# Attention's keys and values in their own memory, and the group normalisation beside the first attention heads

## What is computed

```
# group B, last steps, per head
mu = hc.mean(-1, keepdims=True)
var = jnp.square(hc - mu).mean(-1, keepdims=True)
hc = (hc - mu) * lax.rsqrt(var + LN_EPS)
h = hc.transpose(0, 2, 1, 3).reshape(B, S, M_WIDTH) * norm_g
return (jax.nn.sigmoid(z.astype(f32)) * h).astype(u.dtype)
...
# group A: c is the normalised latent; keys and values come out of it by w_uk and w_uv
logits = q . key - slope * distance   (unpicked keys masked)
p = softmax(logits);  o = p . value
...
mix = jnp.concatenate([a_out, m_out], axis=-1) @ w_out[l]
h = layer_norm(DN_ALPHA * h + mix, ln1_g[l], ln1_b[l])
```

## Time and profile before

| what | value |
| --- | --- |
| median of 3 runs | 2743.13 us (2736.57 to 2743.91) |
| the profiled execution's own time | 2728.71 us |
| its span in the profile | 2726.9 us |
| its mean granted clock | 0.952 |
| PE busy / DVE / ACT / POOL | 92% / 65% / 51% / 11% of the span |

### The profile page before, as it was taken

The page is one execution under the profiler, slowest core; times in us unless marked ns, Lnnn a source line. Parts: engine busy times, 40 slices in busy tenths (PEclk is TensorE's granted clock), DMA queues, the critical chain, the costliest instruction groups (busy, mean ns, idle before and its releaser), DMA issues.

```text
span 2726.9 us, 37894 instructions
## 1 busy us (share of the span) xinstructions
PE 2496.0 (92%) x11204; PEld 1797.3 (66%) x11205; DVE 1762.2 (65%) x2804; ACT 1393.3 (51%) x2029; POOL 301.4 (11%) x233
## 2 busy tenths in 40 slices
PE   7999987898976999999999999999999999999991
PEld 3544456576543777777777777777777777777770
DVE  0476865453445655768867687668769669557596
ACT  0378525552111444647646575546557557346473
POOL 0003722002000000101101001100100100001012
PEclk9999998998995999999999999999999999999995
DMA  4100020002033555859957697667859859557583
GB/s 154 62 4 31 0 108 1 1 1 86 0 129 135 177 165 183 280 177 314 309 177 268 214 329 268 219 230 266 273 193 337 270 190 337 186 186 265 189 302 144
DMA packets 81644, 488.48 MB, mean 179 GB/s; under 512 B 13683, under 2 KB 14963, under 8 KB 30454
## 3 DMA queue, kind: packets, MB, share of 16 engines
q1 hardware_dynamic: 66512, 449.67, 46.1%
q0 software_dynamic: 13104, 34.11, 5.5%
q10 hardware_dynamic: 1974, 4.02, 0.5%
HBM read 465.42 MB, written 36.70 MB: 184 GB/s over the span
## 4 chain that ended last, share of the span: by engine, by line
PE 72%; DVE 14%; issue 9%; ACT 2%; DMA 2%; DVEq 0%; POOL 0%; POOLq 0%; ACTq 0%; SPq 0%
PE ps L777 15%; PE ps L778 14%; PE ps L779 14%; DVE wlo L1559 8%; PE ps L523 7%; PE ps L534 5%; PE ps L702 4%; PE ps L798 2%; PE ps L684 2%; PE ps L808 2%; PE ps L665 1%; PE ps L552 1%; PE ps L672 1%; PE ps L764 1%; PE ps L595 1%
## 5 line engine op out<-in xcount | busy, mean ns | idle before, releaser
L1559 DVE TENSOR_TENSOR wlo<-raw,whi 128x1024 fp32r<-128x1024 f32 x776 | 935.8, 1221 | 283.5 <-ACT whi L1065 257.3
L1065 ACT ACTIVATE whi<-raw 128x1024 fp32r<-128x1024 f32 x776 | 820.2, 1061 | 465.9 <-PE ps L779 439.6
L777 PE MATMUL ps<-whi,xhi 128*128 128x512 f32 x1440 | 595.8, 414 | 0.0
L778 PE MATMUL ps<-wlo,xhi 128*128 128x512 f32 x1440 | 575.9, 400 | 0.0
L779 PE MATMUL ps<-whi,xlo 128*128 128x512 f32 x1440 | 572.8, 398 | 0.0
L777 PEld LDWEIGHTS ps<-whi,xhi 128*128 128x128 f32 x1440 | 277.7, 193 | 97.2 <-issue 36.2
L779 PEld LDWEIGHTS ps<-whi,xlo 128*128 128x128 f32 x1440 | 278.2, 193 | 62.0
L778 PEld LDWEIGHTS ps<-wlo,xhi 128*128 128x128 f32 x1440 | 278.7, 194 | 53.0
L777 PE MATMUL ps<-whi,hhi 128*128 128x512 f32 x720 | 296.0, 411 | 0.0
L779 PE MATMUL ps<-whi,hlo 128*128 128x512 f32 x720 | 282.9, 393 | 0.0
L778 PE MATMUL ps<-wlo,hhi 128*128 128x512 f32 x720 | 280.7, 390 | 0.0
(11 more groups left out here) (312 smaller groups left out, 2686.0 us busy)
## 6 DMA issues: line engine op xcount, KB each, us to landing
raw<-in_w_gu SPq DMA_DIRECT2D x260, 1024.0 KB, 5.3
raw<-in_w_dn SPq DMA_DIRECT2D x128, 1024.0 KB
xT<-in_xT SPq DMA_DIRECT2D x2, 2048.0 KB, 15.9
raw<-in_w_out SPq DMA_DIRECT2D x2, 2048.0 KB
h1all<-in_x SPq DMA_DIRECT2D x4, 1024.0 KB, 8.0
hext<-h1all SPq DMA_DIRECT2D x8, 512.0 KB, 11.9
acc<-accst SPq DMA_DIRECT2D x8, 512.0 KB, 2.6
fin<-acc SPq DMA_DIRECT2D x2, 2048.0 KB, 13.2
```

Of the source, the lines that this page charges most:

```text
L777: pe.matmul(bank_ap, hi, whi[:, slot, col, :], start=start, stop=False)
L778: pe.matmul(bank_ap, hi, wlo[:, slot, col, :], start=False, stop=False)
L1065: act.activation(whi[:, j % 2, 2 * g:2 * g + 2, :], raw[:, (j + 2) % 3, 2 * g:2 * g + 2, :], ACT.Copy)\
L1559: dve.tensor_tensor(wlo[:, j % 2, s, :], raw[:, (j + 2) % 3, s, :], whi[:, j % 2, s, :].bitcast(f32), ALU.subtract).then_inc(lo_done, 1)
```

## The change

`Vn` goes to the memory of slot 2 of `raw` (address 32 KB instead of that of `vaug`), and `KTr` to that of `ucT`, the recurrence's input, which is dead by then. `w_gu[0]` therefore can't be loaded before attention has ended: its two halves are issued behind `bsrc`. On PE the `kt` and `V` tasks follow the recurrence at once, and the eight `mt` tasks are done at n = 6, 8, ... 20 of attention. On ACT the copies of `KTr` come ahead of the root, and the 32 normalising instructions follow two by two behind the exponential and the copy of n = 0 to 15. On DVE the copies of `Vn` come ahead of the reciprocal, and the copy of `mt` chunk c is the last thing of iteration n = 6 + 2c. POOL's program is the same.

```diff
+TURN_AT = tuple(range(6, 6 + 2 * NT, 2))
...
-        Vn = at("Vn", X + 102, [P, NT, AH * AD])
-        KTr = at("KTr", X + 118.5, [P, 4, S])
+        Vn = at("Vn", 32, [P, NT, AH * AD])
+        KTr = at("KTr", X + 86, [P, 4, S])
...
-            filled(sp, last_use[5])
-            half_slabs(0, a["w_gu"][0])
...
             sp.dma_start(bsrc[:, :], a["b_gu"]).then_inc(bias_all_in, 16)
+            half_slabs(0, a["w_gu"][0])
...
+                if n in TURN_AT:
+                    c = TURN_AT.index(n)
+                    b = opened(("mt", c))
+                    pe.wait_ge(mout, c + 1)
+                    for h in range(MH):
+                        ins = pe.transpose(b[:, h * P:(h + 1) * P], zs[:, c, h, :], ident)
+                    closes(ins, ("mt", c))
...
+                if n == 0:
+                    act.wait_ge(mnorm_in, 2)
+                for c, h in (divmod(2 * n, MH), divmod(2 * n + 1, MH)) if n < 2 * NT else ():
+                    act.activation(vaug[:, c, h, 0:MD], vaug[:, c, h, 0:MD], ACT.Identity,
+                                   scale=m_rstd[:, c, h:h + 1], bias=m_nmr[:, c, h:h + 1]).then_inc(mnormed, 1)
```

More of the change, by code:

```diff
@@ L76, in task_order @@
         o += [("U", c, q) for q in range(2) if c < NT - 1]
-    o += [("mt", c) for c in range(NT)]
     o += [("kt", m, n) for n in range(2) for m in range(4)] + [("V", t) for t in range(NT)]
@@ L85, in task_order @@
             o += [("at", n // AH - 1)]
+        if n in TURN_AT:
+            o += [("mt", TURN_AT.index(n))]
     for t in range(NT):
@@ L632, in _ @@
                     closes(ins, ("U", c, q))
[L633 to L638, removed]
             for j in range(2):
@@ L982, in _ @@
                     copy_out(("X", c, q), mst[:, h, :], b[:, 129:258], scale=gate_cols[:, 1, h * 8 + c:h * 8 + c + 1])
[L983 to L989, removed]
             for n in range(2):
@@ L992, in _ @@
                     copy_out(("kt", m, n), KTr[:, m, n * 512:(n + 1) * 512], filled(act, ("kt", m, n))[:, :])
+            act.wait_ge(mvar_done, 1)
+            act.activation(m_rstd[:, :, :], m_rstd[:, :, :], ACT.Sqrt).then_inc(mroot, 1)
             for n in range(NT * AH + 4):
@@ L1365, in _ @@
             dve.tensor_scalar(m_rstd[:, :, :], m_mv[:, :, :, 1], EPS, None, ALU.add).then_inc(mvar_done, 1)
+            for t in range(NT):
+                b = filled(dve, ("V", t))
+                frees(dve.tensor_copy(Vn[:, t, :], b[:, :]), ("V", t))
             dve.wait_ge(mroot, 1)
@@ L1370, in _ @@
                                      op0=ALU.mult, op1=ALU.mult).then_inc(mnorm_in, 1)
[L1371 to L1377, removed]
             astep = serial(dve, att_step)
@@ L1408, in _ @@
                                       att_rec[:, :].unsqueeze(2).to_broadcast([P, AH, AD]), ALU.mult).then_inc(o_copied, 1)
+                if n in TURN_AT:
+                    c = TURN_AT.index(n)
+                    b = filled(dve, ("mt", c))
+                    frees(dve.tensor_copy(catT[:, 4:8, c * P:(c + 1) * P], b[:, :].rearrange("p (h d) -> p h d", h=4)),
+                          ("mt", c))
             lstep = serial(dve, ln_step)
```

## The result

| kernel | median | ratio to before (95% interval) |
| --- | --- | --- |
| before | 2740.31 us (2736.57 to 2743.91, 6 runs) | |
| changed | 2727.55 us (2719.87 to 2729.74, 6 runs) | 0.9949 (0.9939 to 0.996) |

The change is worth 12.8 us, 0.5%; the prediction had 9.4. The time forecast was 2733.7 us; of the 6.1 us between it and the measured 2727.55, 2.8 lie in the median of before, which was 2743.13 over three runs and is 2740.31 over six. The profiled execution of the changed kernel has a span of 2724.5 us and took 2726.3, not the 2719.3 of the forecast: the profiled execution of before was a short one, as a second trace of it shows further down. The three terms are read from the two traces as distances, since the recurrence itself ends up to 4 us apart from one execution to the next (454.2 to 458.5 us in the traces of this study).

What follows compares the result with a forecast made beforehand. The prediction took the chain of waits between recurrence and output projection as the bound; 20.3 - 5.4 - 5.5 = 9.4 us gained, so 2743.1 - 9.4 = 2733.7 us, range 2726 to 2742.

Steps and rivals of the forecast that it cites:

- Term 1: Start of attention: keys follow the recurrence at once, normalisation leaves the path, first exponential comes earlier; gain of 20.3 us.
- Term 3: Wait before the projection: moved `w_gu[0]` takes DMA turns ahead of ACT's five small loads; 5.5 us lost.
- the bounds: Limits on the moved load's cost before the projection: 0 if ACT's loads pass first, 6.0 us at most.
- Term 2: Attention: normalisations and transposed blocks now lie in iterations 0 to 20; 5.4 us lost.
- the prediction's own sign: Attention, first exponential to last product: Term 2 is wrong if it grows by under 3 or over 9 us.
- 1.0 for the clock: Attention, change from tile 0 to 1: more transposes fall in the half-clock stretch, at twice their time; 1.0 us lost.
- It becomes the bound by 0.43 us for 4 pairs: Attention tile 0: ACT needs 2.66 us per pair of heads against 2.23; 1.7 us lost.
- 0.5 x 4 pairs = 2.0 us in tile 1: Attention tile 1: transposed blocks make odd exponentials 3.5 us apart in place of 3.01; 2.0 us lost.
- The hidden load: Before the projection: ACT's five loads don't wait for `w_gu`; gain 14.9 us, time 2728 us; chance 0.15.
- The blocked port: Attention: POOL's multiplications stop DVE's small step, costing 9.4 us; nothing left of the gain, about 2743 us; chance 0.25.
- the slower rival: Attention: PE's clock stays at half through tiles 2 and 3; 18 us slower than before, 2761 us; chance 0.05.

Runs made afterwards that it cites:

- The block's return: Changed kernel, but ACT's 32 normalisations stand in one block ahead of the first exponential, as before the change: 2740.42 us, ratio 0.9998.
- Load taken back: Changed kernel, but SP issues `w_gu[0]` only after ACT's five small loads have landed: 2722.31 us, ratio 0.9937.
- load alone: Kernel before, with only `w_gu[0]` moved, to behind `bsrc` instead of ahead of attention: 2744.74 us, ratio 1.0023.
- attention without guests: Kernel before, with PE waiting for ACT's five loads only ahead of the first router product; no normalisations or transposed blocks in attention: 2724.53 us, ratio 0.995.
- the two kernels with the blocks in late tiles: Changed kernel with the eight transposed blocks at n = 40 to 54: 2738.39 us; the same with DVE's copy one iteration later: 2729.06 us.
- the late wait: PE waits for ACT's five loads only ahead of the first router product: 2707.59 us on the changed kernel, 2724.53 us on the kernel before.

## Why the prediction was right, and where it was off

**Term 1** held, step by step: keys at once, 13.8 us for keys and values at full clock, both table loads beside the values, and DVE's reciprocal and shift laid bare (0.5 us, from 471.56 to 472.05; 0.6 predicted). The block's return shows that 13.3 of the 20.6 us are ACT's block with the table load behind it; the others come from the order of PE's work and the kept clock, which no run takes apart.

**Term 3** held. Load taken back and load alone show its cause and its size: 4.1 and 5.3 us in PE's wait, 5.2 and 4.6 us in the medians. That it was met to 0.1 us in the first pair of traces is luck, since the wait scatters by 2 us. The choice between the bounds, by the packets and not the bytes, was right: nearly all of `w_gu` went by before `br` was through, not the 1.33 MB that equal turns in bytes would allow. That the queues take turns packet by packet is what the Trainium skill, DMA: Bandwidth & Descriptors, section on queues, rings and completion order, says; the 273 and 279 packets of the two queues agree.

**Term 2** is the step that was mis-sized: 5.4 predicted, 3.2 against the first trace of before and 1.4 against the others. By the prediction's own sign (attention longer by under 3 us) it was wrong against all but the first trace. By tiles 0, 1 and 2 attention lost 2.2, 0.9 and 0.1 us against the first trace and 1.1, 0.1 and 0.1 against the second; 1.9, 2.0 and 0.5 were predicted, and 1.0 for the clock. Three parts of it:

- "It becomes the bound by 0.43 us for 4 pairs" in tile 0: true only of the first pair (0.56 us). The other pairs ran at half clock, where PE sets 2.85 us, above ACT's 2.66. The same 2.85 stands in attention without guests. The first trace of before, whose clock stayed at full for 7.3 us behind the first exponential, was the exception among the four traces with that attention (2.6 to 3.1 us in the others), and I took it for the rule. That the sum for tile 0 comes near the measured 2.2 us is luck: most of that is the clock.
- "0.5 x 4 pairs = 2.0 us in tile 1": from one odd exponential to the next, from n = 9 on, it is 3.49, 3.54, 3.41 and 3.56 us, as worked out (3.5). But the 3.01 us that I set against it was one pair of the four; before, they took 3.67, 3.50, 3.01 and 3.47. Only that one pair lost clearly, 0.4 us, and by its transposed block: in the two kernels with the blocks in late tiles it takes 3.05 us. Why the others were long before as well was not taken apart.
- The price of one transposed block isn't a constant: 0.2 us for five of them from n = 12 to 24, 1.46 us each in tiles 5 and 6. Had the change put them late, my sum of PE's time would have missed two thirds of it.

The overall step is thus one of reading: a pair is costed against the rows of its own place, and a single trace doesn't show where the clock falls in the next execution.

**The rivals.** The hidden load fell with the two load experiments. What the prediction held against it, that ACT's packets at the program's start were large, doesn't follow from its rows: 0.98 MB in 720 packets is 1.4 KB each there, 1.33 MB in 624 is 2.1 KB each here. The blocked port didn't come about: the small step that it would have stopped took at most 218 ns, and POOL's eight multiplications their usual 1.18 us:

```profile
L1389 DVE TENSOR_SCALAR att_bias<-att_m x64: 212/214/218, 472.3 to 628.2; 128x1 f32<-128x1 f32 x64
...
L1703 POOL TENSOR_TENSOR zs<-vaug,zs x8: 1178/1180/1185, 475.2 to 498.8; 128x512 f32<-128x512 f32 x8
```

In this trace only one of these steps runs beside a multiplication (at 478.06 us, 214 ns), but in the other traces with the work in attention 65 more do, and none takes over 215 ns. The step has one tensor input; that of the earlier trace rows has two. The clock did fall early, as the slower rival had it, but rose again in tile 1, and was at 1.00 for the rest of attention.

## What to carry to other kernels

Work of an idle engine hides well beside a stage that another engine bounds, but look at what stands behind each wait that you insert on an in-order engine: the same eight copies cost next to nothing in one place and 1.46 us each in another, and 9 us came back by moving the waiting copy one step down. A load that is moved to make room should be followed to the transfers that it now shares the queues with, and from there to the engine that waits. And when a wait grows, ask first whether that engine reads the data at all.

## What was not expected of the hardware

The granted clock falls at a different point of the same program in different executions: 7.3 us behind the first exponential in the first trace of before, 3.1 us in the second, 2.6 in the kernel before with the late wait, whose instructions up to there are the same. It then stays at half for 6.8 us in the first and for 13.7 us in the others. That goes with 1.8 us of attention (152.7 and 154.5).

The late wait gained more than its 15.0 us of tail: 20.0 us between the medians (2727.55 and 2707.59), and 15.8 in the kernel before, where the tail gives 8.8 to 9.7. In the four traces with it the experts' loop took 1848 to 1852 us, with 1853 to 1857 in all others but the first of before (1847). The loop's length goes with its clock. The time at half speed in it, summed from each trace's records of the granted clock, is 130 us in the first trace of before, 140 in the two of 1848 and 1849 us, 147 to 150 in those of 1851 to 1853, and 151 to 155 in those of 1855 to 1857. Whether the earlier, gapless projection brings the shorter time at half speed about, or the scatter of executions, was not tried and stays open.
